# Sparse attention on one core: the rule that interleaves scored heads and turned blocks is counted in true columns

## The reference, cut to what matters

```python
p_c = masked_softmax(einsum('tghd,cgd->tghc', qg, kc), mask_c)      # compressed keys, 63 of them
o_c = einsum('tghc,cgd->tghd', p_c, vc)
...                                                                  # 16 blocks of 64 keys: all of them
p_s = masked_softmax(einsum('tghd,tgkpd->tghkp', qg, kg), mask_s)   # selected keys
o_s = einsum('tghkp,tgkpd->tghd', p_s, vg)
p_w = masked_softmax(einsum('tghd,wgd->tghw', qg, kw), mask_w)      # window of 512 back
o_w = einsum('tghw,wgd->tghd', p_w, vw)
o = gb[..., 0:1] * o_c + gb[..., 1:2] * o_s + gb[..., 2:3] * o_w
```

## Time and profile before

| | |
|---|---|
| median of 3 runs | 1710.82 us (1710.09 to 1714.05) |
| the profiled execution | 1708.87 us |
| its span, first to last instruction | 1707.1 us |
| its mean granted TensorE clock | 0.992 |
| sparse attention in it: first key product of head 0 to the first product behind the stage | 139.41 to 431.46 us |

### The profile page before, as it was taken

One profiled execution on the slowest core, in us unless ns is written; L12 is line 12 of the kernel. 1 busy time (PEld: TensorE's weight loads), 2 busy tenths in 40 slices (PEclk: granted clock), 3 DMA queues, 4 the chain that ended last, 5 costly groups with the idle time before them and its releaser, 6 DMA issues.

```text
span 1707.1 us, 22658 instructions
## 1 busy us (share of the span) xinstructions
PE 1639.1 (96%) x8238; PEld 1360.6 (80%) x8238; DVE 1223.7 (72%) x1592; ACT 723.6 (42%) x1388; POOL 878.7 (51%) x678
## 2 busy tenths in 40 slices
PE   7998899988999998999999999999999999999997
PEld 6886778776788887889888788878788888887886
DVE  6864678776877788447446536878888788788965
ACT  5124678876233234135223205344444444443444
POOL 3333445443423342412323553489987888789841
PEclk9999999999999999999999999999999999999999
DMA  5130111110111114134100241244543544784432
GB/s 192 62 120 26 50 38 31 33 39 12 50 50 50 38 61 149 74 120 163 34 31 26 87 148 62 93 144 171 170 158 121 167 156 148 262 290 157 142 112 99
DMA packets 80331, 176.47 MB, mean 103 GB/s; under 512 B 7836, under 2 KB 24412, under 8 KB 80096
## 3 DMA queue, kind: packets, MB, share of 16 engines
q1 hardware_dynamic: 67944, 135.71, 23.9%
q10 hardware_dynamic: 12280, 39.34, 6.2%
HBM read 136.21 MB, written 38.81 MB: 103 GB/s over the span
## 4 chain that ended last, share of the span: by engine, by line
PE 52%; DVE 17%; POOL 13%; ACT 9%; issue 8%; DMA 1%; ACTq 0%; SPq 0%; POOLq 0%; DVEq 0%
PE ps L1110 13%; PE ps L1113 13%; PE ps L1114 13%; DVE x_t L2996 4%; PE ps L1310 3%; POOL sum_s L1021 2%; ACT x_t L2199 2%; POOL w_lo L1015 2%; POOL w_lo L1071 2%; DVE x_t L3025 2%; POOL s_new L1041 1%; POOL spare_lo L1071 1%; ACT pt_hi L1885 1%; ACT probs L1865 1%; PE ps L1332 1%
## 5 line engine op out<-in xcount | busy, mean ns | idle before, releaser
L1110 PE MATMUL ps<-h_hi,w_hi 128*128 128x512 f32 x1060 | 419.5, 396 | 10.2 <-POOL h_lo L999 3.2
L1114 PE MATMUL ps<-h_hi,w_lo 128*128 128x512 f32 x1060 | 414.9, 391 | 0.0
L1113 PE MATMUL ps<-h_lo,w_hi 128*128 128x512 f32 x1060 | 414.8, 391 | 0.0
L920 POOL TENSOR_TENSOR w_hi<-w_raw,ones 128x1024 fp32r<-128x1024 f32 x52 | 109.8, 2111 | 509.6 <-PE ps L1110 425.6
L1110 PEld LDWEIGHTS ps<-h_hi,w_hi 128*128 128x128 f32 x1060 | 200.2, 189 | 59.7 <-ACT p_sum L2168 8.0
L1114 PEld LDWEIGHTS ps<-h_hi,w_lo 128*128 128x128 f32 x1060 | 200.1, 189 | 42.6
L1113 PEld LDWEIGHTS ps<-h_lo,w_hi 128*128 128x128 f32 x1060 | 200.3, 189 | 39.7
L959 POOL TENSOR_SCALAR probs<-probs,nsa_inv,gate_sig 128x640 f32<-128x640 f32 (+7 forms) x128 | 100.8, 787 | 154.1 <-DVE nsa_inv L2588 153.7
L2996 DVE SCALAR_TENSOR_TENSOR x_t<-ps,par,x_t 128x1023 f32<-128x1023 f32 x84 | 107.7, 1282 | 73.0 <-ACT x_t L2199 71.5
L925 POOL TENSOR_TENSOR w_lo<-w_raw,w_hi 128x1024 fp32r<-128x1024 f32 x52 | 138.1, 2656 | 4.0
L2371 DVE TENSOR_TENSOR pt_lo<-ps,pt_hi 128x512 fp32r<-128x512 f32 (+6 forms) x148 | 101.7, 687 | 50.0 <-ACT pt_hi L1885 47.3
(11 more groups left out here) (412 smaller groups left out, 4084.2 us busy)
## 6 DMA issues: line engine op xcount, KB each, us to landing
w_raw<-in_w_tiles SPq DMA_DIRECT2D x109, 512.0 KB, 3.4
w_raw<-in_w_tiles SPq DMA_DIRECT2D x55, 256.0 KB, 3.0
s_new<-in_w_tiles SPq DMA_DIRECT2D x44, 256.0 KB, 4.1
z_dram<-x_t ACTq DMA_DIRECT2D x21, 512.0 KB, 2.9
b<-z_dram SPq DMA_DIRECT2D x33, 256.0 KB, 3.8
q_st<-q_dram SPq DMA_DIRECT2D x64, 128.0 KB, 2.9
x_dram<-x_t ACTq DMA_DIRECT2D x14, 512.0 KB, 2.8
t_dram<-t_new ACTq DMA_DIRECT2D x22, 256.0 KB, 5.5
```

Source lines behind the costliest of these rows:

```text
L920: pool.tensor_tensor(w_hi[s][:, :], w_raw[s][:, :], ones[:, :].to_broadcast([P, KT * P]), ALU.mult).then_inc(w_hi_made.sem, w_hi_made.up())
L1110: ins = mm(out_ap, whi, x_hi, start=first, stop=False)
L1113: mm(out_ap, whi, x_lo, start=False, stop=False)
L1114: return mm(out_ap, wlo, x_hi, start=False, stop=last)
```

## The change

The rule counts other columns. Before, every "p" step counts as 4 x 128 columns turned, the narrow compressed ones too, and each head of branch 1 counts as its key blocks plus `DH` = 64 columns scored, whatever the number of its compressed keys. After, a step counts as its own width times four (`step_cols`) and a head as its own columns (`part_cols`), and `T_LAG` is 3584 instead of 2560. All else stays: the same heads, the same steps, the same order within each, the same places in `probs`.

```diff
-T_LAG = 2560
+T_LAG = 3584
...
+def step_cols(k):
+
+    kind, s, a = STEPS[k]
+    if kind == "o":
+        return 0
+    _, i, _, _, n = part_of(s)
+    return GH * (P if a < n else seen_cmp(i))
+
+
 def nsa_order():
 
     order, done, scored, turned = [], 0, 0, 0
     for j in range(HEADS):
         while done < P_FREE[j]:
-            turned += STEPS[done][0] == "p" and GH * P
+            turned += step_cols(done)
             order.append(("k", done))
             done += 1
         order.append(("s", j))
-        _, _, br, _, n = part_of(j // GH)
-        scored += n * P + DH * br
+        scored += part_cols(j // GH)
         burst = 0
         while done < len(STEPS) and burst < 3:
             kind, s, _ = STEPS[done]
-            if kind == "p" and (GH * s + GH + SCALE_LAG > j or turned + GH * P > scored - T_LAG):
+            if kind == "p" and (GH * s + GH + SCALE_LAG > j or turned + step_cols(done) > scored - T_LAG):
                 break
-            turned += kind == "p" and GH * P
+            turned += step_cols(done)
             order.append(("k", done))
             done += 1
             burst += 1
```

## The result

The changed kernel takes 1714.43 us (median of 20 runs, 1709.72 to 1721.18), the kernel before 1711.81 us (20 runs beside them, 1709.64 to 1714.05). The ratio is 1.0015 with a 95% interval of 1.0009 to 1.0021: 2.6 us slower. I had forecast 0.6 us less and a change too small to tell. The time lies in my range and the size within my "same", but the sign is wrong: the interval excludes both my -0.6 us and no change at all.

What follows compares the result with a forecast made beforehand. TensorE was taken to bound the stage's middle, three-engine chains its borders; -0.4 - 0.9 + 1.8 + 3.2 + 1.8 - 3.6 + 2.8 - 5.3 = -0.6 us against 1710.82 gave 1710.2 us, range 1704.8 to 1715.2.

Steps and rivals of the forecast that it cites:

- The reading of the stage: Sparse attention: TensorE bounds its middle; at borders of wide and narrow heads, chains through three engines do (head 30 waits 2.22 us).
- Heads 8 to 15 and 16 to 23: Early blocks one head later, -0.4 us in the first window; two steps fewer at half price, -0.9 in the second.
- heads 104 to 111: A burst of five steps gets spread, as in the equally wide heads 16 to 23: -3.6 us, to 11.1.
- The end: From head 120 on, five "p" and one "o" leave the tail, one of each joins narrow heads: -5.3 us.
- a 'p' step where PE is the bound costs it 0.90 us, start to start: Price per moved step, used for two more steps (+1.8 us) in several windows and six more in heads 112 to 119.
- Heads 24 to 31: Window that gets two more steps, 15 instead of 13: +1.8 us.
- Heads 112 to 119: Priced from equally wide heads 8 to 15, with two new bare heads that wait long: +2.8 us, to 26.4.
- rival 2: Bare heads 116 and 117 don't stall, as nine steps in front give PE a backlog: 1705.6 us, chance 0.16.
- The bare heads: Heads 32 to 95: six heads without a step behind them instead of two, four more at 0.35 us: +1.4 us.
- Rival 3: Single bare heads 45, 85, 101 wait 2.2 us, then low clock, 3.5 us each; two make 1717.3 us; chance 0.08.
- Rival 4: Order hardly matters, PE catches up; only the tail's 0.13 us per step counts: -0.8, 1710.0 us; chance 0.02.
- the first one: The forecast itself: gains at the burst and in the tail eaten by new bare heads, 1710.2 us; chance 0.74.

Runs made afterwards that it cites:

- the kernel with at most two: The changed kernel with at most two steps behind a head instead of three: 1717.60 us, ratio 1.0036 to the kernel before.
- the late part: The kernel before up to head 95, with the changed kernel's cumulative steps from head 96 on: 1712.68 us, ratio 1.0012 to the kernel before.

## Why the prediction was wrong

**The reading of the stage** was right. The chain at a bare head was the one I read from the earlier trace rows: taking the maximum out from behind the low half took 1.5 us off the wait before head 30 and 1.4 off the longest one of the earlier trace rows (0.5 of it came back before head 14). It showed more than I had made of it: a gain of 7.0 us in the median lay there, which has nothing to do with the distance that the change holds.

**Heads 8 to 15 and 16 to 23** came as forecast, a little better (-0.86 and -1.06 against -0.4 and -0.9). So did **heads 104 to 111**, -3.90 against -3.6: the twin window of the same widths was a good measure. **The end** gave 4.66 us instead of 5.3; the granted clock was 0.91 in its last 13.78 us, against 1.00 before.

**The step that failed** is the price "a 'p' step where PE is the bound costs it 0.90 us, start to start", taken for heads 24 to 31, 32 to 95, 96 to 103 and 112 to 119. The earlier trace rows are two of the three steps behind head 15, just after PE's long waits had let ScalarE and VectorE catch up, and there the price holds. In a row of wide heads that all have two steps, PE is not the bound. The chain of after behind heads 98 and 99 shows it; the lines are head 98's maximum and exponentials, a copy out, the high halves of two steps, the low half of the first of them, head 99's maximum, and PE's next turn:

```profile
354.23 1.07 DVE L2583 TENSOR_REDUCE nsa_shift<-ps 128x1 f32<-128x896 f32 x1
...
355.39 1.01 ACT L1873 ACTIVATE probs<-ps,nsa_shift 128x896 f32<-128x896 f32 x1 [1.09 <-DVE nsa_shift L2583]
...
356.39 0.59 ACT L1901 ACTIVATE o_turn<-ps 128x512 f32<-128x512 f32 x1
...
356.87 1.08 ACT L1893 ACTIVATE pt_hi<-ps 128x512 fp32r<-128x512 f32 x2
357.50 0.69 DVE L2379 TENSOR_TENSOR pt_lo<-ps,pt_hi 128x512 fp32r<-128x512 f32 x1 [1.60 <-ACT pt_hi L1893]
...
358.18 1.07 DVE L2583 TENSOR_REDUCE nsa_shift<-ps 128x1 f32<-128x896 f32 x1
...
358.24 0.66 PE L1318 MATMUL ps<-ident,probs 128*128 128x128 f32 x4 [1.04 <-DVE pt_lo L2379]
```

VectorE stood idle for 1.60 us until the high half at 356.87, which stood behind the exponentials; head 99's maximum stood behind that low half, and PE waited 1.04 us. Per head this chain is maximum, exponentials, high and low half, 1.07 + 1.01 + 0.54 + 0.68 = 3.3 us and the gaps between; from head 98's maximum to head 99's it was 3.95. PE's own time is 2.7 us a head (10.68 / 4, heads 96 to 99 with 2,2,1,2 steps, PE idle for 0.05). With 2,2,2,3 steps these heads took 3.66 us each, PE idle for 1.75 of the 14.63. The same shows in heads 24 to 27: 10.57 us with 2,2,1,2 steps, 12.50 with 2,2,2,2 (the kernel with at most two) and 14.12 with 2,2,2,3. So the two-deep buffers hide the chain with two such heads in a row and not with four; where the border lies was not measured. A step in such a row cost 1.7 (heads 24 to 27), 2.0 (96 to 99), 1.2 (112 to 115) and, net of the step taken away elsewhere, 0.87 too much (76 to 83). **Heads 24 to 31** hid the same error: two steps more behind heads 26 and 27 made the first four heads 3.55 us longer (14.12 us against 10.57), and a low stretch of the clock that did not come, 1.7, gave half of it back.

**Heads 112 to 119** I had priced at +2.8 from their twin window. The stall and its clock came, so rival 2 fell, but the low stretch lasted 6.6 us and not 3.4, worth 1.6 us (the late part, with the same steps in these heads, had 3.4 and took 28.20 us, so this share of the miss differs between executions), and heads 112 to 115, with 2,3,2,2 steps, are one of the rows above: heads 8 to 11, from which I had worked, had only three steps. A twin in width is no twin when the steps behind its heads differ.

**The bare heads** between 32 and 95 I had as +1.4 by their waits. Behind the six of after PE waited 3.0 us in all (1.06 us at the most, before head 35), behind the two of before 0.74: +2.3, within the bounds. The sum of that window was +4.27 against 3.2, and the largest parts of it sit where three steps stand at the border of a part: +2.52 in heads 40 to 47 and +3.22 in heads 80 to 87, for one step more in each, while other windows lost steps and time. There the failure of the price is the third step's as much as the row's: head 83's cost 2.0 us. Rival 3, a clock that falls at the single bare heads 45, 85 and 101, did not occur in the profile: the waits before heads 46, 86 and 102 were 0, 0.11 and 0.59 us, and from head 24 to head 111 the clock was 1.00 in every window.

**Rival 4**, that only the tail counts, fell with the sum. I had added it to the first one's chance; a rival in which the steps cost more than 0.90 where they were put had no place in my list at all, and that is the one that happened.

**What stays open.** In the two profiles the stage is 5.0 us longer, but the whole only 2.6; I had let the stage's shift pass to the end whole. So my sum missed the stage by 5.6 us, and that the difference of the medians missed by no more than 3.2 is luck, for no run shows where the rest went. The stage began 1.16 us earlier in after (138.25 against 139.41), and what follows it took 1.3 us less. The other kernels began between 138.2 and 139.5 with nothing changed ahead of the stage, so the first looks like a difference between executions; for the second I have no cause that a run shows. What a third step costs by itself, apart from a bare head behind it, is open too.

## What to carry to other kernels

An order shared by several engines has a price per entry only as long as one engine is the bound of that stretch; behind each wide entry add up the longest serial chain through the others as well, and compare it with the bound's own time before you move work in. A constant distance between producer and consumer evens out the columns and not the chain: what helped here was, in most places, no more than two wide heads in a row with two steps, and a step left over for the heads that would have had none; the two were not tested apart. And where two instructions of one engine stand in an arbitrary order, look which of them another engine waits for; swapping them at the one kind of place where it mattered was worth 7 us, and everywhere it cost 8 to 9.

## What the runs showed of the hardware

The granted clock fell behind a stretch in which PE was busy for 3.24 of 6.07 us, and stayed at the lower level (1.2 GHz) for 6.6 us although PE was busy all through. The late part, with the same steps and the same wait there (2.25 us), had 3.4 us of it. In before, the low stretches in the stage had 3.4 us each. And like waits need not have like clocks: before head 30, PE waited 2.22 us in before and 2.23 in after, and the window had 0.93 in the one and 1.00 in the other. This did not vary within a kind: all three profiles with before's list in these heads have 0.93, both with after's 1.00. So a term of the sum that holds a low stretch is uncertain by its 1.7 us, however well its wait is known. The spread between executions of one and the same kernel goes largely with the clock: of the 20 runs of after, the fastest (1709.72 us) had a mean clock of 0.995, the highest of all, and the slowest (1721.18 us) 0.986, the lowest.
